# Modulation sums of 128x512 with the column halves on the partition halves, and trigonometry at other slabs

## The reference

```python
    c_act = jax.nn.silu(c)                                   # c: 1024 values
    mod = jnp.dot(c_act, ada_w[l]) + ada_b[l]                # 1024 x 6144 weights, 6144 sums
    sh1, sc1, g1, sh2, sc2, g2 = jnp.split(mod, 6, axis=-1)
    h = modulate(rms_norm_2(x, norm1_g[l]), sh1, sc1)        # h * (1 + scale) + shift
    qa = rope(split_heads(aq, A_HEADS, A_HEAD_DIM), positions)   # cos and sin of position * frequency
```

## Time and profile before

| | us |
|---|---|
| median of 3 runs | 895.03 (894.59 to 895.73) |
| the profiled execution | 894.6 |
| its span in the profile | 893.3 |
| PE busy | 882.8 (99%) |
| DVE busy | 730.5 (82%) |
| ACT busy | 569.7 (64%) |

### The profile page before, as it was taken

How to read it: one execution, slowest core, us unless ns; L and a number is a source line. 1 busy time by engine, 2 the same in 40 slices (tenths; PEclk the granted TensorE clock), 3 DMA queues, 4 the chain that set the end, 5 groups by cost and what they waited for, 6 DMA issues and landing times.

```text
span 893.3 us, 18500 instructions
## 1 busy us (share of the span) xinstructions
PE 882.8 (99%) x7368; PEld 859.7 (96%) x7368; DVE 730.5 (82%) x1164; ACT 569.7 (64%) x834; POOL 1.9 (0%) x9
## 2 busy tenths in 40 slices
PE   9999999999999999999999999999999999999996
PEld 7999989999999999999999999999999999999995
DVE  6778998899998899898965999998788885555554
ACT  7848456776586787664446868667785664444541
POOL 0000000000000000000000000000000000000000
PEclk9999999999999999999999999999999999999999
DMA  8766456455875789998856566654545666666641
GB/s 314 262 190 226 152 153 201 147 186 209 293 259 186 265 290 340 357 334 312 330 180 203 165 204 197 199 160 127 169 146 183 192 203 194 197 195 196 186 150 48
DMA packets 53157, 189.83 MB, mean 213 GB/s; under 512 B 6208, under 2 KB 6864, under 8 KB 52944
## 3 DMA queue, kind: packets, MB, share of 16 engines
q1 hardware_dynamic: 52928, 188.65, 64.4%
q10 hardware_dynamic: 144, 0.00, 0.0%
HBM read 186.53 MB, written 1.05 MB: 210 GB/s over the span
## 4 chain that ended last, share of the span: by engine, by line
PE 97%; ACT 1%; DMA 1%; DVE 1%; issue 0%; SPq 0%; ACTq 0%
PE bank L1016 28%; PE bank L1019 28%; PE bank L1018 28%; PE bank L989 2%; PE bank L991 2%; PE bank L990 2%; DMA H<-in_xT 1%; PE bank L724 1%; PE bank L665 0%; PE bank L961 0%; PE bank L968 0%; PE bank L964 0%; PE bank L827 0%; DVE H L1862 0%; PE bank L579 0%; PE bank L699 0%
## 5 line engine op out<-in xcount | busy, mean ns | idle before, releaser
L1055 DVE TENSOR_TENSOR wlo<-raw,whi 128x1024 fp32r<-128x1024 f32 x297 | 360.5, 1221 | 92.3 <-ACT whi L1918 91.3
L1918 ACT ACTIVATE whi<-raw 128x1024 fp32r<-128x1024 f32 x297 | 311.7, 1057 | 193.5 <-PE bank L1019 180.3
L1016 PE MATMUL bank<-Alo,whi 128*128 128x256 f32 x1344 | 376.0, 280 | 0.0
L1018 PE MATMUL bank<-Ahi,wlo 128*128 128x256 f32 x1344 | 371.9, 277 | 0.0
L1019 PE MATMUL bank<-Ahi,whi 128*128 128x256 f32 x1344 | 371.8, 277 | 0.0
L1016 PEld LDWEIGHTS bank<-Alo,whi 128*128 128x128 f32 x1344 | 252.6, 188 | 2.9 <-issue 2.6
L1018 PEld LDWEIGHTS bank<-Ahi,wlo 128*128 128x128 f32 x1344 | 252.6, 188 | 0.4 <-issue 0.2
L1019 PEld LDWEIGHTS bank<-Ahi,whi 128*128 128x128 f32 x1344 | 252.5, 188 | 0.0
L1018 PE MATMUL bank<-Fhi,wlo 128*128 128x256 f32 (+1 forms) x320 | 88.8, 278 | 0.0
L1019 PE MATMUL bank<-Fhi,whi 128*128 128x256 f32 (+1 forms) x320 | 88.8, 278 | 0.0
L1016 PE MATMUL bank<-Flo,whi 128*128 128x256 f32 x256 | 70.9, 277 | 0.0
(11 more groups left out here) (408 smaller groups left out, 1377.8 us busy)
## 6 DMA issues: line engine op xcount, KB each, us to landing
raw<-in_stream SPq DMA_DIRECT2D x298, 512.0 KB, 4.3
araw<-in_ada SPq DMA_DIRECT2D x48, 512.0 KB, 6.0
TB<-in_TB SPq DMA_DIRECT2D x1, 1536.0 KB, 7.2
a8r<-a SPq DMA_DIRECT2D x16, 64.0 KB, 3.8
bc<-in_bc SPq DMA_DIRECT2D x1, 896.0 KB, 6.0
out<-H SPq DMA_DIRECT2D x3, 256.0 KB, 2.2
H<-in_xT SPq DMA_DIRECT2D x1, 512.0 KB, 7.5
mats<-in_mats SPq DMA_DIRECT2D x1, 449.0 KB, 7.1
```

The source lines that it names most:

```text
L1016: pe.matmul(os[j], wh, xl, start=k == 0 and (wide or j == 0), stop=False, skip_group_check=not wide)
L1018: pe.matmul(os[j], wl, xh, start=False, stop=False, skip_group_check=not wide)
L1055: v.tensor_tensor(wlo[:, s % NHL, :], raw[:, s % NRAW, :], whi[:, s % NHL, :].bitcast(F32), ALU.subtract).then_inc(*lo_v.up(s))
L1918: a.activation(whi[:, s % NHL, :], raw[:, s % NRAW, :], ACT.Copy).then_inc(*hi.up(s))
```

## The change

The modulation weights are laid out otherwise. Before, partition i of a step holds row 128 k + i with 1024 columns. After, a step's 1024 columns are two halves h; partitions 64 h to 64 h + 63 hold half h, and each partition has two rows (i and 64 + i), 512 columns of each, one beside the other. So a step loads by two DMAs, each to 64 partitions with rows of 512 values; DVE takes two instructions of 128x512 in a row, the second of which waits for the first, with a scalar for each of the two rows (`csil` has 16 columns, in a buffer of its own that was a gap, and is filled by four small DMAs at the start); the sum is 128x512, PE turns it with four transposes into bank 6, and DVE adds 64 columns per result, in two reductions with a stride. The results land in the same places of `mod`. Apart from that the trigonometry's steps move to slabs 122 to 132 on DVE and 128 and 134 on ACT.

```diff
--- before.py
+++ after.py
@@ -189,7 +189,7 @@
             [n for h in range(4) for n in (45 + 6 * h, 49 + 6 * h, 50 + 6 * h)]),
     "conv": ([73, 78.5], [*(n for n in range(18, 70) if n not in (36, 41, 63, 64)), 72, 75, 76, 79, 80, 81, 82, 83],
              [73, 75, 78, 79, 80, 81, 82]),
-    "trig": ([], [98, 100, 102, 104, 106, 108], [104, 110]),
+    "trig": ([], [122, 124, 126, 128, 130, 132], [128, 134]),
     "ada": ([], ADA, [58]),
     "sums": (SUMS, [n + 1 for n in SUMS] + [SUMS[5] + 3], []),
     "r2": ([98], [96, 100, 101], [98]),
@@ -306,7 +306,7 @@
         shb = sb("shb", [128, 8])
         spare = sb("spare", [128, 1])[:, :]
 
-        sb("gap0", [128, 16])
+        csil = sb("csil", [128, 16])
         Ahi = sb("Ahi", [128, KD, T], F32R)
         Alo = sb("Alo", [128, KD, T], F32R)
         t512 = [sb(f"t512_{i}", [128, 512]) for i in range(2)]
@@ -367,7 +367,7 @@
         p2.close()
         posi, ki = ple[:, 0, :].bitcast(I32), ple[:, 1, :].bitcast(I32)
         ang, kf, pT = ple[:, 2, :], ple[:, 3, :], ple[:, 4:6, :]
-        g2, csil = modg[:, 16:24], shb
+        g2 = modg[:, 16:24]
         aacc = (aacc0, aacc1)
         aw2 = nrm[:, 0:2 * T]
         xb_ = Fhi[:, :, :].rearrange("p a t -> p (a t)")[:, 0:24 * T].rearrange("p (h k t) -> p h k t", h=2, k=8)
@@ -444,8 +444,8 @@
         raw_in = signals(" ".join(f"raw{i}" for i in range(NRAW)))
         x_in = signals("x0 x1 x2")
         ar_in = signals("ar0 ar1 ar2")
-        g1_in, cols_in, mats_in, bc1_in, sgw_in, wa2_in, tb_in, pos_in, pT_in, bc2_in, stored = signals(
-            "g1 cols_l mats_l bc1_l sgw_l wa2_l tb_l pos_l pT_l bc2_l stored")
+        g1_in, c_in, cols_in, mats_in, bc1_in, sgw_in, wa2_in, tb_in, pos_in, pT_in, bc2_in, stored = signals(
+            "g1 c_l cols_l mats_l bc1_l sgw_l wa2_l tb_l pos_l pT_l bc2_l stored")
 
         hi, lo_v, mm, drained_s, drained_v = signals("hi lo_v mm drained_s drained_v")
 
@@ -505,8 +505,11 @@
                         w.wait_ge(*gla_s.at("hi", 3))
                         w.wait_ge(*gla_v.at("lo", 3))
                         w.wait_ge(*gla_pe.at("o", 1))
-                    sp.dma_start(araw[:, n % 3, :], A["ada"][n % 8, :, (n // 8) * 1024:(n // 8) * 1024 + 1024]
-                                 ).then_inc(*ar_in[n % 3].up(n, by=16))
+                    for h in range(2):
+                        c0 = (n // 8) * 1024 + 512 * h
+                        sp.dma_start(araw[64 * h:64 * h + 64, n % 3, :].rearrange("i (b j) -> i b j", b=2),
+                                     A["ada"][n % 8, :, c0:c0 + 512].rearrange("(b i) j -> i b j", b=2)
+                                     ).then_inc(*ar_in[n % 3].up(n, by=16))
 
             def ada():
                 fetch(0)
@@ -539,6 +542,10 @@
             load_slab(5)
             sp.dma_start(mats[:, :], A["mats"]).then_inc(*mats_in.up("in", by=16))
             load_slab(6)
+            for h in range(2):
+                for b in range(2):
+                    sp.dma_start(csil[64 * h:64 * h + 64, 8 * b:8 * b + 8],
+                                 A["cols"][64 * b:64 * b + 64, COFF["c"]:COFF["c"] + 8]).then_inc(*c_in.up("in", by=16))
 
             for name in NAMES:
                 if name == "gq":
@@ -720,8 +727,8 @@
                         w.wait_ge(*red_v.at(cb - 1))
                     else:
                         w.wait_ge(*att_s.at("p", 3, 1))
-                    for j in range(8):
-                        i = pe.transpose(banks[6 + j // 4][:, j % 4 * 128:j % 4 * 128 + 128],
+                    for j in range(4):
+                        i = pe.transpose(banks[6][:, j * 128:j * 128 + 128],
                                          aacc[cb % 2][:, j * 128:j * 128 + 128], ident)
                     i.then_inc(*ada_pe.up(cb))
                     plain(5)
@@ -1369,26 +1376,31 @@
                 w.wait_ge(*ada_s.at("c"))
                 for cb in range(6):
                     for k in range(8):
-                        n, o = 8 * cb + k, aacc[cb % 2][:, :]
+                        n, o = 8 * cb + k, aacc[cb % 2][:, 0:512]
                         w.wait_ge(*ar_in[n % 3].at(n))
                         if k == 0:
                             if cb >= 2:
                                 w.wait_ge(*ada_pe.at(cb - 2))
                             elif cb:
                                 w.wait_ge(*mm.at("wo", 3))
-                            v.tensor_scalar(o, araw[:, n % 3, :], csil[:, k:k + 1], None, ALU.mult).then_inc(*ada_v.up(n))
+                            v.tensor_scalar(o, araw[:, n % 3, 0:512], csil[:, k:k + 1], None, ALU.mult
+                                            ).then_inc(*ada_v.up("first", n))
                         else:
                             w.wait_ge(*ada_v.at(n - 1))
-                            v.scalar_tensor_tensor(out=o, in0=araw[:, n % 3, :], scalar=csil[:, k:k + 1], in1=o,
-                                                   op0=ALU.mult, op1=ALU.add).then_inc(*ada_v.up(n))
+                            v.scalar_tensor_tensor(out=o, in0=araw[:, n % 3, 0:512], scalar=csil[:, k:k + 1], in1=o,
+                                                   op0=ALU.mult, op1=ALU.add).then_inc(*ada_v.up("first", n))
+                        w.wait_ge(*ada_v.at("first", n))
+                        v.scalar_tensor_tensor(out=o, in0=araw[:, n % 3, 512:1024], scalar=csil[:, 8 + k:9 + k], in1=o,
+                                               op0=ALU.mult, op1=ALU.add).then_inc(*ada_v.up(n))
                         yield
 
             def sums():
                 for cb in range(6):
                     w.wait_ge(*ada_pe.at(cb))
-                    for j in range(2):
-                        i = v.tensor_reduce(mod[:, 8 * cb + 4 * j:8 * cb + 4 * j + 4],
-                                            banks[6 + j][:, :].rearrange("p (a c) -> p a c", a=4), AXX, ALU.add)
+                    for h in range(2):
+                        i = v.tensor_reduce(mod[:, 8 * cb + 4 * h:8 * cb + 4 * h + 4],
+                                            banks[6][:, :].rearrange("p (a h c) -> p a h c", a=4, h=2)[:, :, h, :],
+                                            AXX, ALU.add)
                     i.then_inc(*red_v.up(cb))
                     yield
                 w.wait_ge(*red_v.at(5))
@@ -2074,7 +2086,8 @@
                     yield
 
             def ada():
-                a.activation(csil[:, :], cols[:, COFF["c"]:COFF["c"] + 8], ACT.Silu).then_inc(*ada_s.up("c"))
+                w.wait_ge(*c_in.at("in"))
+                a.activation(csil[:, :], csil[:, :], ACT.Silu).then_inc(*ada_s.up("c"))
                 yield
 
             def r2():
```

## The result

The kernel after takes 958.29 us (median of 4 runs, 947.33 to 961.52) against 894.94 us of before: a ratio of 1.0675, 95% interval 1.0621 to 1.0728. Forecast was 896.6 us. It is slower by 63 us, and the forecast missed it. The other three were 9 to 14 us longer at a mean granted clock of 0.975 to 0.979 (0.985 in the profiled one), which by an estimate from these clocks is 6 to 9 us of it; where the rest went is not shown.

A forecast was written before the change was run, and what follows sets the result against it. TensorE, busy 99% of the span, was taken as the bound, with VectorE nearly late in feeding it; stretches of +0.75, -0.88 and +1.7 us summed to +1.6 on 895.03, so 896.6 us, 8-in-10 range 892.3 to 908.

The forecast's parts named there:

- the sum of +1.6 us: Whole kernel: +0.75 us at slabs 66 to 83, -0.88 at 97 to 121, +1.7 at 122 to 149.
- rival (a): Modulation loads to 64 partitions become the bound, deciding above 1.9 us of DMA time per load; 908 us, chance 0.30.
- The price of 908 us: Slabs 301 to 447 us: half the doubling, 29 us added, 17 too many, less 6 of cushion: +11 us.
- The reckoning at full cost (46 us): From 301 to 447 us: half-partition loads hold the engines twice as long, 58 us added, stretch 46 us too short.
- The split step: VectorE's two 128x512 multiply-adds, the second waiting, hold the queue 1.45 us for 1.19: +0.26 in each of 42 steps.
- Four transposes for eight: TensorE in each of six blocks: four transposes fewer, 24 x 0.11 = 2.64 us, the whole gain.
- The 10.4 us: Net work added on VectorE: 10.9 for split steps plus 2.8 for first steps less 3.3 for reductions.
- the first block's stall: Slabs 66 to 83: PE waits 0.65 us at slab 83 and is 1.2 us late in all by the transposes.
- the stalls before transposes: Slabs 122 to 149: PE 2.2 us late at the transposes due at 449.81 us, as step 47 ends at 452.0.
- The walk: VectorE's queue, slabs 122 to 149: 9.6 us added, 6.1 us absorbed by gaps, 3.5 us remain.
- the wait through ScalarE: Slab 128: ScalarE's sine delays a copy for the embedding, so VectorE's instruction at 394.15 waits, 1.2 us more.
- Rival (b): The saving comes through: split steps cost +0.13 us and the sine fits ScalarE's gaps; -2.6 us, 892.7 us, chance 0.20.

The follow-up runs named there:

- one_load: The changed kernel with modulation weights laid out ahead so each step is one DMA to all 128 partitions, 4 KB rows: 902.09 us, ratio 1.0081.
- before_trig: The kernel before with only the trigonometry moved to the change's slabs (122 to 132 on VectorE, 128 and 134 on ScalarE): 896.63 us, ratio 1.0015.
- no_plain: one_load with the trigonometry moved to slabs 150 to 157 and no plain product behind each block's four transposes: 895.31 us, ratio 1.0008.
- turn_twice: one_load with the trigonometry moved to slabs 150 to 157 and each of a block's four transposes made twice: 896.35 us, ratio 1.0017.
- all_2k: As one_load, but each step loaded by two DMAs to all 128 partitions, 512 columns each, 96 issues with 2 KB rows: 906.26 us, ratio 1.0121.

## Why the prediction was wrong

**The step that failed** is the one that left the loads' share of the DMA engines at what it was: the 96 halves were charged for their issue and for 0.3 us of later landing, and the sum of +1.6 us ran over PE and VectorE alone. A pair of halves to partitions 0 to 63 and 64 to 127 costs the stretch 3.2 us of the engines' time, not 1.46: some 2.3 of its own, and the rest by what it adds to the slabs beside it. The decision point that rival (a) gave, 1.9 us, was right, and the trace after shows what it named: landings well over 6 us, a DMA share near 1, VectorE and ScalarE waiting for DMA. By the Trainium skill ("SBUF — State Buffer", section "Door 1: The DMA port swizzle") the ports that a DMA reaches depend on its partitions: 0 to 63 reach eight of sixteen. By its formula, in which the two lowest bits of the partition's number don't change the port, all even or all odd ones reach all sixteen. The traces agree in what follows for the times, 12.4 us to landing for the one and 5.0 for the other; the ports themselves are not in them.

**Its chance and its price were too low as well.** Against (a) stood that the issues are half as large and that no load to 64 partitions was to be seen in the trace; neither is a reason that such a load should be cheap. And there was a faint sign: the trace of before has DMAs to 32 partitions (`a8r`, from 555 to 581 us) whose 2 KB packets took 117 ns on average, where those of the last outputs took 87. At 0.90 a resource has room for a tenth more, and the modulation loads were 58 of its 134 us: a rise by 30% of their cost (1.9 for 1.46) decides. The price of 908 us came from halving the doubling, since loads of neighbouring halves might overlap, and from 6 us of cushion. Little of that was found: what a pair costs the stretch rose to 2.2 times, not to 1.5 or 2. Between slabs 98 and 150 the change lost 48 us for the 11 priced. The reckoning at full cost (46 us) was close, in part by luck, as it doubled the halves and left the slabs beside them alone; even its end, 935, lies below the 958.29 measured.

**Steps that held.** The split step: 1.45 us to the next instruction, +0.26, exactly as read from one pair. Four transposes for eight, 24 for 48. VectorE's work in sum: its busy time rose by 7.9 us in one_load, where it hardly waits. The 10.4 us counted the queue, which includes a gap of 0.04 us inside each of 48 pairs, so 8.5 of busy time were to be expected. (The 10.0 us of after look closer and are not: there waits take away the overlap of instructions.)

**Steps that held only in size, or by half.** With the loads mended (one_load) the first block's stall was 0.6 us for 1.2. At slabs 122 to 149 the stalls before transposes were 2.5 us for 2.2, but that they agree is luck: the large one was put at the sixth block's transposes (449.81 us), and it stood at the fifth (426.57), 2.0 us. The walk had taken the whole stretch's gaps as one sum, though several of them lie behind the fifth block and can't help it. (That sum was a little short, too: 6.5 less 1.3 plus twelve times 0.09 is 6.3, not 6.1.) What the trigonometry brings there by itself, 5.1 us against 6.1 of gaps and 1.2 for the wait through ScalarE, was about right: before_trig stalls PE for 0.9 us, again at the fifth block and just before it.

**What was not in it at all**: the pace of the products. Every difference was worked out at 2.72 us a slab; at one clock, with no wait, it can be 2.83. Where small instructions were taken from PE's stream the forecast counted their own 0.11 us each, and with the loads mended they took 5 to 8 us with them. Rival (b), the saving of 2.6 us, is not seen in any kernel: no_plain, which takes out 36 small instructions, is level with before, and its profile loses 3.7 us to slow slabs.

Open: what sets the pace. It changes mostly at small instructions or waits, in turn_twice once amid products; neither the count of transposes, nor a plain product behind them, nor the place decides it alone. It also varies between executions of one kernel: the 29 runs of before fall into a group at 894.1 to 895.1 us and one at 895.7 to 896.4 (one run took 901.55), which would be some 14 slabs at the slow pace, but no profile shows it.

## What to carry to other kernels

Where a relayout narrows a load to half the partitions, ask which half before anything else: price the load by the partitions that it reaches, not by its bytes, and hold it against the DMA share of the stretch, at full price and with a margin, as the loads beside it slow down too. If two halves must come in two DMAs, cut them so that each reaches both the lower and the upper 64 partitions, or lay the data out ahead so that one DMA fills all 128. A forecast that takes a few instructions out of TensorE's stream should carry a tolerance for the pace of what follows (4% here), and its check is the count of matmuls in a fixed window, not the busy time.

## What the runs showed of the hardware

- A load of 512 KB as two DMAs: to even and odd partitions 5.0 us to landing and no cost to the kernel; to the lower and upper 64, 12.4 us and 58 us on the kernel. The loads beside it suffer as much: raw slabs to all 128 partitions land after 14.1 us for 5.9. In the kernel after, their 4 KB packets took 262 ns on average for 179, and the 2 KB packets of the halves 146 for 95 in all_2k.
- 2 KB rows in 96 issues instead of 4 KB in 48, all to 128 partitions: at most 4 us of 900 (all_2k against one_load).
- TensorE starts 128x256 products every 113.3 or every 117.8 ns at a granted clock of 1.00 and a busy share of 1 (179 or 172 in 20 us), and keeps the one or the other over some 7 to 80 slabs, mostly until small instructions or a wait. What sets it is open.
- About a microsecond behind a stall of PE of 3.05 us the granted clock fell from 2.4 to 1.2 GHz for 3.4 us (products 0.21 us apart for 0.12).
